# Setup of a two-block transformer kernel: order of the first loads, who scales the memory rows, and where the sigmoid stands

## What is computed

```python
h = rms_norm(x, mix_norm_g[layer])
proj = h @ w_in[layer]
...
bias = rel_bias[t5_bucket(k_pos[None, :] - q_pos[:, None])]      # diff_attention
lam = jnp.exp(jnp.sum(lp[0] * lp[1])) - jnp.exp(jnp.sum(lp[2] * lp[3])) + lam_init
...
def memory_attention(h, mem, mem_g, w_q, w_kv, q_g, k_g, w_o):
    m = rms_norm(mem, mem_g)
    kv = (m @ w_kv).reshape(b, n, 2, MEM_HEADS, MEM_DIM)
...
def second_block(x, c, ada_w, ada_b, ...):
    cond = jax.nn.silu(c)
    for i in range(DEPTH):
        mod = (cond @ ada_w[i] + ada_b[i])[:, None, :]
```

## Time and profile before

| | us |
|---|---|
| median of 3 runs | 2587.52 |
| lowest, highest | 2587.31, 2588.34 |
| the profiled execution's own time | 2589.35 |
| its span | 2587.6 |
| busy: PE, DVE, ACT, POOL | 2556.5, 1140.3, 677.0, 1309.8 |
| granted TensorE clock, mean | 0.999 |

### The profile page before, as it was taken

The page is one execution under the profiler, slowest core; times in us unless marked ns, Lnnn a source line. Parts: engine busy times, 40 slices in busy tenths (PEclk is TensorE's granted clock), DMA queues, the critical chain, the costliest instruction groups (busy, mean ns, idle before and its releaser), DMA issues.

```text
span 2587.6 us, 35508 instructions
## 1 busy us (share of the span) xinstructions
PE 2556.5 (99%) x14691; PEld 2048.2 (79%) x14691; DVE 1140.3 (44%) x1983; ACT 677.0 (26%) x1333; POOL 1309.8 (51%) x546
## 2 busy tenths in 40 slices
PE   7999999999999999999999999999999999999998
PEld 6877668888888876688888867888888888888887
DVE  4345464666533445656665345322224135322224
ACT  5245451111022454511111344200001333300002
POOL 5543236665565432355565733566665522555553
PEclk9999999999999999999999999999999999999999
DMA  8321133565332111345553211322223211232221
GB/s 261 84 60 35 32 114 118 191 195 194 115 98 82 60 50 33 98 146 184 182 187 114 85 50 33 117 94 94 96 97 98 82 50 34 82 98 97 97 97 65
DMA packets 222509, 265.38 MB, mean 103 GB/s; under 512 B 19248, under 2 KB 197000, under 8 KB 222248
## 3 DMA queue, kind: packets, MB, share of 16 engines
q1 hardware_dynamic: 219648, 256.58, 31.0%
q10 hardware_dynamic: 2728, 6.90, 0.8%
HBM read 258.74 MB, written 4.72 MB: 102 GB/s over the span
## 4 chain that ended last, share of the span: by engine, by line
PE 97%; DVE 1%; DMA 1%; ACT 0%; SPq 0%; issue 0%; DVEq 0%; PEldq 0%; PEld 0%
PE PS L990 10%; PE PS L993 10%; PE PS L994 10%; PE PS L1724 5%; PE PS L938 5%; PE PS L943 5%; PE PS L942 5%; PE PS L1728 4%; PE PS L1727 4%; PE PS L1244 1%; PE PS L1248 1%; PE PS L1247 1%; PE PS L2018 1%; PE PS L1007 1%; PE PS L1853 1%; PE PS L1280 1%
## 5 line engine op out<-in xcount | busy, mean ns | idle before, releaser
L845 POOL TENSOR_SCALAR WH<-RAW 128x2048 fp32r<-128x2048 f32 x178 | 341.7, 1920 | 1061.8 <-issue 911.1
L847 POOL TENSOR_TENSOR WL<-RAW,WH 128x2048 fp32r<-128x2048 f32 x178 | 822.6, 4621 | 14.9
L990 PE MATMUL PS<-Hh,WL 128*128 128x512 f32 x1152 | 448.6, 389 | 0.0
L993 PE MATMUL PS<-Hl,WH 128*128 128x512 f32 x1152 | 448.2, 389 | 0.0
L994 PE MATMUL PS<-Hh,WH 128*128 128x512 f32 x1152 | 448.1, 389 | 0.0
L2724 DVE SCALAR_TENSOR_TENSOR X<-PS,X 128x512 f32<-128x512 f32 x304 | 208.6, 688 | 189.6 <-PE PS L1728 127.7
L994 PEld LDWEIGHTS PS<-Hh,WH 128*128 128x128 f32 x1152 | 216.2, 188 | 45.2
L990 PEld LDWEIGHTS PS<-Hh,WL 128*128 128x128 f32 x1152 | 216.2, 188 | 45.2 <-issue 0.4
L993 PEld LDWEIGHTS PS<-Hl,WH 128*128 128x128 f32 x1152 | 216.2, 188 | 44.7
L3110 DVE TENSOR_TENSOR PS<-SQ,PS 128x512 f32<-128x512 f32 x44 | 30.6, 696 | 427.2 <-PE PS L994 427.2
L1724 PE MATMUL PS<-U,WL 128*128 128x512 f32 x512 | 202.3, 395 | 0.0
(11 more groups left out here) (554 smaller groups left out, 4681.5 us busy)
## 6 DMA issues: line engine op xcount, KB each, us to landing
RAW<-in_w_ff SPq DMA_DIRECT2D x64, 1024.0 KB, 5.2
PROJ<-in_ada_w SPq DMA_DIRECT2D x48, 1024.0 KB, 8.0
RAW<-in_ffn_w_in SPq DMA_DIRECT2D x44, 1024.0 KB, 5.1
RAW<-in_ffn_w_out SPq DMA_DIRECT2D x22, 1024.0 KB, 4.9
RAW<-in_w_in SPq DMA_DIRECT2D x20, 1024.0 KB, 5.3
RAW<-in_w_out SPq DMA_DIRECT2D x8, 1024.0 KB, 5.1
RAW<-in_a_w_in SPq DMA_DIRECT2D x6, 1024.0 KB, 4.9
RAW<-in_b_w_in SPq DMA_DIRECT2D x12, 512.0 KB, 4.6
```

The costliest lines, as they stand in the source:

```text
L845: pool.tensor_scalar(WH[b][:, :], RAW[b][:, :], 1.0, 1.0, ALU.mult, ALU.mult).then_inc(s.split_hi, 1)
L847: pool.tensor_tensor(WL[b][:, :], RAW[b][:, :], WH[b][:, :].bitcast(F32), ALU.subtract).then_inc(s.split_done, 1)
L990: ins = mm(bank, WL[b][:, col:col + P], Hh[:, k, :], start=k == 0, stop=False)
L993: mm(bank, WH[b][:, col:col + P], Hl[:, k, :], start=False, stop=False)
```

## The change

SP now asks for the memory rows first, then consts, the first panel, x, and the second panel. Behind a wait on `su_rb` (VectorE's memset of the gain rows, near the start) come the small gain loads, which ScalarE issued before, six of them now as one load with a broadcast instead of two, and ada_b; behind a wait on `x_in` spread, da_lambda, a_sink, trig and rot. ScalarE issues the eight row loads, onehot and rel_bias. `rows_in` counts 8 loads, `small_in` 13.

GpSimd's first two splits don't wait for `panels_begun`. TensorE counts the second panel as begun at the first matmul of `norm_squares(0)` instead of the first matmul of the memory values.

TensorE transposes ada_b and the small gains after the tokens instead of before the memory rows. VectorE copies PA ahead of the reciprocal and scales only the first 128 memory rows; ScalarE scales the others (a Copy with a scale). ScalarE copies the two halves of the bias table between memory tiles, writes the table to DRAM after its last copy of memory tiles, makes NSINK after the squares, and computes silu of c in the first layer, after the normed tiles.

```diff
         def _(sp):
-            sp.dma_start(C[:, :], t["consts"]).then_inc(s.const_in, 16)
-            sp.dma_start(projf[0:32, 6144:6144 + REL], t["onehot"]).then_inc(s.const_in, 16)
-            sp.dma_start(projf[0:32, 6144 + REL:6144 + REL + 8], t["rel_bias"]).then_inc(s.const_in, 16)
             sp.dma_start(projf[:, 4096:6144].rearrange("p (i d) -> p i d", i=MT),
                          t["mem"][0].rearrange("(i p) d -> p i d", p=P)).then_inc(s.mem_in, 16)
...
+            sp.dma_start(C[:, :], t["consts"]).then_inc(s.const_in, 16)
...
             panel(1, 1, KT, 256, t["w_mem_kv"][0, :, 256:512])
+            sp.wait_ge(s.su_rb, 1)
...
+            sp.dma_start(PROJ[0:96, 14, P:2 * P], t["ada_b_2"].rearrange("l (t p) -> (l t) p", p=P)).then_inc(s.small_in, 16)
+            sp.wait_ge(s.x_in, 16)
             sp.dma_start(PTS[:, 1, 0:256].rearrange("p (b c) -> p b c", b=2), t["spread"]).then_inc(s.lam_in, 16)
+            sp.dma_start(PROJ[:, 15, :], t["da_lambda"].rearrange("l r d -> (l r d)").partition_broadcast(P)).then_inc(s.lam_in, 16)
+            sp.dma_start(SINK[:, :, 0], t["a_sink_2"].rearrange("l h -> (l h)").partition_broadcast(P)).then_inc(s.lam_in, 16)
...
                 pool.wait_ge(raw_ready[b], 16 * loads(at))
-                pool.wait_ge(s.panels_begun, at + 2)
+                if at >= 2:
+                    pool.wait_ge(s.panels_begun, at + 2)
...
-            pe.wait_ge(s.rows_in, 16 * 9)
-            pe.wait_ge(s.small_in, 16 * 18)
-            pe.transpose(PS[:, 7, 0:112], PROJ[0:112, 14, 0:P], C[0:112, C_ID:C_ID + 112])
...
+            pe.wait_ge(s.rows_in, 16 * 8)
+            pe.transpose(PS[:, 7, 0:112], PROJ[0:112, 14, 0:P], C[0:112, C_ID:C_ID + 112]).then_inc(s.su_rowc, 1)
...
+            pe.wait_ge(s.small_in, 16 * 13)
+            pe.wait_ge(s.su_pc, 1)
+            pe.transpose(PS[:, 7, 112:208], PROJ[0:96, 14, P:2 * P], C[0:96, C_ID:C_ID + 96])
+            pe.transpose(PS[:, 7, 208:232], PROJ[0:24, 14, 2 * P:3 * P], C[0:24, C_ID:C_ID + 24]).then_inc(s.su_rowc, 1)
...
-            norm_squares(0)
+            norm_squares(0, panel_left=True)
...
+            act.wait_ge(s.su_ri, 1)
+            f(projf[:, 4096 + D:4096 + 2 * D], projf[:, 4096 + D:4096 + 2 * D], ACT.Copy, scale=SM[:, SM_MS + 1:SM_MS + 2]).then_inc(s.su_ri, 1)
             act.wait_ge(s.su_pc, 1)
-            f(SM[:, SM_C:SM_C + KT], PA[:, 104:112], ACT.Silu)
...
                 if L == 0:
+                    f(SM[:, SM_C:SM_C + KT], PA[:, 104:112], ACT.Silu)
                     act.wait_ge(s.skew, 16)
...
-            v.wait_ge(s.su_act, 2 + MT + 1)
+            v.wait_ge(s.su_rowc, 1)
+            v.tensor_copy(PA[:, :], PS[:, 7, 0:112]).then_inc(s.su_pc, 1)
+            v.wait_ge(s.su_act, MT + 1)
             v.reciprocal(SM[:, SM_MS:SM_MS + MT], SM[:, SM_MR:SM_MR + MT]).then_inc(s.su_ri, 1)
             v.wait_ge(s.su_ri, 1)
-            for i in range(MT):
-                row = projf[:, 4096 + i * D:4096 + (i + 1) * D]
-                v.tensor_scalar(row, row, SM[:, SM_MS + i:SM_MS + i + 1], None, ALU.mult).then_inc(s.su_ri, 1)
-            v.wait_ge(s.su_rowc, 1)
-            v.tensor_copy(PA[:, :], PS[:, 7, 0:112]).then_inc(s.su_pc, 1)
+            v.tensor_scalar(projf[:, 4096:4096 + D], projf[:, 4096:4096 + D], SM[:, SM_MS:SM_MS + 1], None, ALU.mult).then_inc(s.su_ri, 1)
```

More of the change, by code:

```diff
@@ L1137, in _ @@
                 if f < 2:
-                    pe.wait_ge(s.su_act, f + 1)
+                    pe.wait_ge(s.su_act, MT + 1 + f + 1)
                 elif f >= 3 and f % 2:
@@ L2264, in root_next @@
                 f(SM[:, SM_MR:SM_MR + 1], eps, ACT.Sqrt)
-            act.wait_ge(s.su_rb, 1)
-            rows_c = PROJ[0:2 * KINDS, 14, 2 * P:3 * P]
-            for k, g in ((K_DAQ, t["da_q_norm_g"]), (K_DAK, t["da_k_norm_g"]), (K_SBO, t["sb_out_g"]),
-                         (K_MLAO, t["mla_out_g"]), (K_MEMQ, t["mem_q_norm_g"]), (K_MEMK, t["mem_k_norm_g"])):
-                for half in range(2):
-                    act.dma_start(rows_c[2 * k:2 * k + 2, HD * half:HD * half + HD], g).then_inc(s.small_in, 16)
-            for k, g in ((K_SUBLN, t["da_subln_g"]), (K_CKV, t["mla_ckv_norm_g"]), (K_CQ0, t["mla_cq_norm_g"][:, 0:P]),
-                         (K_CQ1, t["mla_cq_norm_g"][:, P:2 * P]), (K_MLAQ, t["mla_q_norm_g"]), (K_MLAK, t["mla_k_norm_g"])):
-                act.dma_start(rows_c[2 * k:2 * k + 2, 0:g.shape[1]], g).then_inc(s.small_in, 16)
-            act.dma_start(PROJ[:, 15, :], t["da_lambda"].rearrange("l r d -> (l r d)").partition_broadcast(P)).then_inc(s.lam_in, 16)
-            act.dma_start(SINK[:, :, 0], t["a_sink_2"].rearrange("l h -> (l h)").partition_broadcast(P)).then_inc(s.lam_in, 16)
+            rows_a = PROJ[0:112, 14, 0:P]
+            at = 0
+            for g in (t["mix_norm_g"], t["memx_norm_g"], t["mem_norm_g"], t["ffn_norm_g"], t["norm_mix_2"], t["norm_ffn_2"]):
+                act.dma_start(rows_a[at:at + 16, :], g.rearrange("l (t p) -> (l t) p", p=P)).then_inc(s.rows_in, 16)
+                at += 16
+            act.dma_start(rows_a[96:104, :], t["final_norm_2"].rearrange("(t p) -> t p", p=P)).then_inc(s.rows_in, 16)
+            act.dma_start(rows_a[104:112, :], t["c_2"].rearrange("b (t p) -> (b t) p", p=P)).then_inc(s.rows_in, 16)
+            act.dma_start(projf[0:32, 6144:6144 + REL], t["onehot"]).then_inc(s.const_in, 16)
+            act.dma_start(projf[0:32, 6144 + REL:6144 + REL + 8], t["rel_bias"]).then_inc(s.const_in, 16)
             act.wait_ge(s.const_in, 16 * 3)
             root_next()
-            for half in range(2):
-                act.wait_ge(s.su_t5, half + 1)
-                f(ATT[:, half * REL // 2:(half + 1) * REL // 2], PS[:, 4 + half, 0:REL // 2], ACT.Copy).then_inc(s.su_act, 1)
             act.wait_ge(s.mem_in, 16)
@@ L2310, in _ @@
                 f(MEMT[:, i, :], PS[:, i % BANKS, 0:N_MEM], ACT.Copy)
-            act.wait_ge(s.lam_in, 16 * 5)
-            f(NSINK[:, :, :], SINK[:, :, :], ACT.Copy, scale=-1.0).then_inc(s.nsink, 1)
+            act.dma_start(scratch.rearrange("m (c r) j -> (m c) r j", c=16),
+                          ATT[:, 0:REL].rearrange("p (r j) -> p r j", r=1).to_broadcast([P, 8, REL])).then_inc(s.skew, 16)
             act.wait_ge(s.su_xc, BANKS + KT // 2)
@@ L2318, in _ @@
                 f(squares_all[i], X[:, i, :], ACT.Square).then_inc(s.nsq, 1)
+            act.wait_ge(s.lam_in, 16 * 5)
+            f(NSINK[:, :, :], SINK[:, :, :], ACT.Copy, scale=-1.0).then_inc(s.nsink, 1)
             act.drain().then_inc(s.left_act, 1)
```

30 lines of the change are left out of this document (14 added, 16 removed).

## The result

The kernel after takes 2592.03 us (median of 22 runs, 2590.67 to 2593.16). The kernel before, run beside it, takes 2588.61 (22 runs, 2587.09 to 2589.79). The ratio is 1.0014, 95% interval 1.0008 to 1.0019. So it is slower by 3.4 us: under 0.2%, but the interval excludes no change. I had forecast 1.1 us less.

What follows compares the result with a forecast made beforehand. TensorE was taken to bound the kernel, so only an earlier end of the setup's sums could pay: 34.90 - 1.0 - 0.1, 1.1 us less, 2588.2 against the profiled execution or 2586.4 against the median; range 2583.5 to 2593.0.

Steps and rivals of the forecast that it cites:

- The measure: Setup: the time TensorE's column sums of squares of the tokens end, 34.90 before, after which it runs without notable gaps.
- constants: Setup loads: onehot and rel_bias, moved to ScalarE's ninth and tenth place, land at 9.8 instead of 5.26.
- a sign of being wrong: Setup: constants in by 8 or after 11, x landing after 20, or a wait on lam_in beyond 29.
- rival 1: VectorE's row scaling meets GpSimd's subtraction if constants come after 10.3: sums at 37.0, +2.1, 2589.6; chance 0.27.
- constants + 0.36: Setup: the start of the path to the row scaling, before 2.46 of bias-table matmuls; scaling may begin at constants + 3.9.
- sums that wait for nothing: End of TensorE's setup in rival 1: column sums that need not wait, estimated at 0.6.
- Rival 2: ScalarE's last loads held behind SP's: constants at 17.4, sums at 41.1, +6.2, 2593.7; chance 0.18.
- Rival 3: Constants at 8.7, lam_in by 25, port free: 3.5 less, 2584.0; chance 0.10.
- (c): ScalarE's eight squares before the sums, 4.3 in all, ending at 34.2 before; claimed last at the sums.
- (d): The memory keys: 5.75 of TensorE matmuls between the token transposes and the sums.
- The lambda product, the cast and lam_in: VectorE before the squares: lam_in's loads in at 27.2, product set at 27.6, cast 1.56 to 0.3, first square 28.9.
- TensorE's own path: Memory transposes done at 20.0, then token transposes, two moved transposes and memory keys: 31.8, hidden under squares ending at 33.2.

Runs made afterwards that it cites:

- second split held: Kernel after with consts first on SP, onehot and rel_bias first on ScalarE, and GpSimd's second split waiting for VectorE's da_lambda work: 2586.3 us.
- port free: The scaling first, plus GpSimd's second split waiting for VectorE's lambda product and its reduction: 2585.79 us, ratio to before 0.999.
- constants first: Kernel after with consts, onehot and rel_bias as SP's first three loads: 2587.71 us, ratio to before 0.9997.
- first split held: Kernel after with GpSimd's first split held until the memory rows are scaled: 2590.23 us, ratio to before 1.0006.
- the scaling first: Kernel after, consts leading SP, onehot and rel_bias leading ScalarE, VectorE's copy of PA behind its memory-row scaling: 2586.22 us.

## Why the prediction was wrong

**The measure was right.** The end of the sums carries the whole difference in every trace: own time less that end is 2554.3 to 2554.5 in the traces of after, before and the experiments, both traces of a kernel included, whatever was moved. (With the second split held and with the port free, where GpSimd is later than the sums, the start of the memory values takes their place, 32.85 and 31.03; that gives 2554.5 and 2554.8.)

**The constants: the step that failed.** The term "constants" was mis-sized, and the copy and the three casts that follow it were taken as if nothing could hold them. I had taken 9.8; they were in at 11.83 (12.2 in the second trace), past the 11 that I had named as a sign of being wrong. Issued at 5.26, earlier than my 5.8, rel_bias took 6.57 to land. I had named both ends, 3.6 and 6.4, and chosen the small one "because its load is as small". Size was the wrong likeness. The 3.6 was measured with consts and onehot, 0.67 MB, asked for ahead of it; the 6.4 of a_sink with a panel and x issued around it. Behind mem, consts, two panels and x the second is nearer. The runs bear this out: the same 1 KB took 3.9 on SP with only consts and onehot ahead, 4.6 to 5.0 as ScalarE's second load with consts leading on SP, 5.9 in the same place with the memory rows leading on SP, and 6.5 to 6.9 as ScalarE's tenth, with all of SP's 5.8 MB asked for. Being early on its own queue is not enough; what the other queue has asked for just before counts. With 11.8 my own rule, "constants after 10.3", gave rival 1.

**The port: right mechanism, wrong instruction.** I looked for a meeting with the row scaling alone. Ahead of it on VectorE stand the copy of rel_bias and three casts, all from SBUF to SBUF, 0.21 and 0.48 long before. I had the copy inside "constants + 0.36" and the casts at nothing, though my own listing of the order shows both. With the constants at 11.83 and GpSimd from 11.67 they meet both of its instructions. Constants at 9.8 would have let them through, and only the scaling would have met GpSimd. The Trainium skill, "SBUF — State Buffer", section "Who interferes with whom", names copy and cast beside tensor_scalar as able to take the shared pair, and says that whoever issues first blocks the other. The trace agrees on both: casts of 4.80 instead of 0.48 behind GpSimd, and a high part of 2.15 instead of 1.90 where VectorE was first (constants first).

**Rival 1 then came out in its numbers, in part by luck.** Transposes 19.6 (measured 19.85 and 19.49), tokens 24.6 (24.96), sums 37.0 (37.38 and 37.58). The start of the transposes fits because the casts waited for the end of the same subtraction for which rival 1 had the scaling wait. From the tokens to the end of the sums two errors cancel: my 5.57 for the token transposes was 4.40 here, and my 0.6 for "sums that wait for nothing" was 1.89. All four terms add up to 12.42 in the rival and in the trace. It gave +2.1 against a trace whose x was late; against the 34.2 of the median it is +2.8, and 3.4 was measured. It should have been the forecast, with 0.27 far too little. Rival 2 was half right: SP was held for 6.79, but ScalarE's issues were not. Rival 3 fell with the constants.

**What bound the sums.** I wrote that the squares (c) were last at the sums in the kernel before. They were not, though nearly: the 64 matmuls run in 1.88 there. In the three kernels where the squares do bind (first split held, constants first, the scaling first) the last 32 alone take 1.93 to 1.99 instead of 1.06. It was (d), the keys. The last four squares, before:

```profile
32.01 2.17 ACT L2318 ACTIVATE HF<-X 128x512 f32<-128x512 f32 x4
```

And after:

```profile
32.82 2.17 ACT L2317 ACTIVATE HF<-X 128x512 f32<-128x512 f32 x4
```

They end at 34.18 and 34.99. The sums end 0.72 and 2.39 later, and only 0.49 later where the squares bind (31.28 and 31.77 in the scaling first). So by these rows the squares had a slack of 0.2 in the kernel before and 1.9 in the kernel after (my estimate). The lambda product, the cast and lam_in, to which I gave a long paragraph, lay under that slack, and the 1.25 that the cast "gave back" was worth nothing here; but with 0.2 of slack the same chain binds as soon as TensorE comes earlier, as the scaling first showed. My sum had TensorE's own path, 31.8, "hidden under the squares", 33.2, but that path was still without the 1.88 of the sums, with which it ends at 33.7. I was also 3.4 too late with lam_in (23.8, not 27.2): SP was free at 12.23 instead of 13.8, the small loads were issued at 0.26 each, most of them, not 0.4, and rot landed in 5.6.

**Tokens and panel.** x landed at 16.4, at my fast end, not 17.8; the first split began at 11.67, 11.30 in the second trace, where I had 12.25. Each was an extra margin on the cautious side. On the port the cautious side was the wrong one: from 11.85 the copy and the casts need 0.6 when nothing holds them, so a split at 12.25 comes behind the copy and meets at most the casts, and one at 11.67 is ahead of them all.

**What was foreseen and held.** The cast of spread takes 0.29. The squares of the memory rows start with the constants (11.96), so asking for those rows first bought nothing. The sigmoid is free:

```profile
51.07 1.28 ACT L2336 ACT_TABLE_LOAD   x1
...
55.77 0.60 ACT L2178 ACTIVATE PROJ<-PS 128x512 f32<-128x512 f32 x1 [1.05 <-PE PS L980]
```

Two table loads and the sigmoid stand ahead of the row at 55.77, and ScalarE is still idle for 1.05, where it had 2.55 in the earlier trace rows. The time stayed inside my range, 2583.5 to 2593.0; its direction did not.

## What to carry to other kernels

When a change makes an engine that shares a port start earlier, list everything that its neighbour has queued from then on, not only the instruction that the diff names, and place the neighbour's start against that list. In these runs a load of 1 KB landed later the more had been asked for around it (3.4 to 6.9 us): load what the setup waits for ahead of the large transfers. And when a chain's start in one trace is a transfer, take a second trace before building on its landing time.

## What the runs showed of the hardware

- One load of 1 KB took from 3.4 us (before, second trace) to 6.9 (after, second trace), with more asked for ahead of it in the second; as second entry of its own queue it still took 5.9 beside the memory rows.
- A copy of 32x128 and three casts of 128x128, 0.7 us of work, held a chain for 6.5 us.
- In the same place, GpSimd first costs VectorE up to the whole rest of the instruction (4.3 us for the casts), VectorE first costs GpSimd 0.15 to 0.35 (2.05 to 2.15 instead of 1.90, 4.85 instead of 4.50), somewhat less than what was left of the VectorE instruction.
- The landing of a 2 MB load issued at 7.49 to 8.32 varied from 19.56 to 21.66, from issue to landing 11.9 to 13.3.
- TensorE's 128x128 transposes of float32 came four per half microsecond and then seven, with a granted clock of 1.00 throughout, and the change came 2 us apart in two executions of one kernel.
